# Kernel for two hybrid transformer layers on one core: seven slots instead of six in the ring of projection weights, with one piece each of q and v handled ahead

## The reference, cut to what matters

```
h = rms_norm(x, norm_g)
z = h @ w_in                         # 1024 x 3624
q, k, v, ga, qi, wi, ki, ub, gb, cv, cg, gc = split_columns(z)
q, k = partial_rope(rms_norm(q)), partial_rope(rms_norm(k))
uc = cv * sigmoid(cg)
att  = attention over the top 132 keys (64 for samples), chosen by
       sum_h wi * relu(qi . ki)       # 8 index heads of 32
pool = windowed means of ub, minus ub, times pool_w
conv = silu(layer_norm(31-tap depthwise conv(uc)))
x = x + concat(att * silu(ga), pool * silu(gb), conv * silu(gc)) @ w_out
```

## Time and profile before

| | us |
|---|---|
| median of 3 runs | 876.19 (873.66 to 878.19) |
| the profiled execution | 876.71 |
| its span, first to last instruction | 875.4 |
| TensorE busy (share of the span) | 805.3 (92%) |
| VectorE busy | 609.3 (70%) |
| ScalarE busy | 328.0 (37%) |
| POOL busy | 333.1 (38%) |

### The profile page before, as it was taken

One profiled execution on the slowest core, in us unless ns is written; L12 is line 12 of the kernel. 1 busy time (PEld: TensorE's weight loads), 2 busy tenths in 40 slices (PEclk: granted clock), 3 DMA queues, 4 the chain that ended last, 5 costly groups with the idle time before them and its releaser, 6 DMA issues. The chain is left out here.

```text
span 875.4 us, 13288 instructions
## 1 busy us (share of the span) xinstructions
PE 805.3 (92%) x4620; PEld 637.6 (73%) x4620; DVE 609.3 (70%) x1432; ACT 328.0 (37%) x830; POOL 333.1 (38%) x317
## 2 busy tenths in 40 slices
PE   5898989999889899999998899899998889999998
PEld 4894635568767777789998655455877777678998
DVE  3546997999998974433444879989999898531122
ACT  3735335336653331223132444343484524122102
POOL 0033886934744700110110568886274373000000
PEclk9999989999889998999999999999999899799999
DMA  4533040314143633012134304002414154400212
GB/s 166 154 99 100 16 121 13 84 42 124 49 113 94 203 124 123 1 44 81 61 101 113 100 4 121 24 21 83 144 52 106 53 163 143 144 1 23 71 54 98
DMA packets 57283, 75.09 MB, mean 86 GB/s; under 512 B 13233, under 2 KB 32889, under 8 KB 57185
## 3 DMA queue, kind: packets, MB, share of 16 engines
q1 hardware_dynamic: 57106, 74.17, 27.7%
q10 hardware_dynamic: 111, 0.08, 0.0%
HBM read 67.26 MB, written 7.61 MB: 86 GB/s over the span
## 5 line engine op out<-in xcount | busy, mean ns | idle before, releaser
L1164 PE MATMUL R<-x_hi,W_r 128*128 128x268 f32 x448 | 141.1, 315 | 27.2 <-DVE yT L1668 7.9
L1148 PE MATMUL R<-W_r,x_hi 128*128 128x512 f32 (+3 forms) x320 | 127.8, 399 | 12.2 <-DVE W_r L1474 12.2
L1177 PE MATMUL R<-yT,W 128*128 128x268 f32 (+2 forms) x768 | 135.0, 335 | 2.4 <-DVE yT L1474 2.4
L1166 PE MATMUL R<-x_hi,W_r 128*128 128x268 f32 x448 | 136.0, 304 | 0.0
L1165 PE MATMUL R<-x_lo,W_r 128*128 128x268 f32 x448 | 135.7, 303 | 0.0
L1177 PEld LDWEIGHTS R<-yT,W 128*128 128x128 f32 x768 | 114.8, 201 | 16.0 <-DVE yT L1474 2.6
L1149 PE MATMUL R<-W_r,x_hi 128*128 128x512 f32 (+3 forms) x320 | 120.7, 377 | 0.0
L1164 PEld LDWEIGHTS R<-x_hi,W_r 128*128 128x128 f32 x448 | 92.2, 206 | 38.9 <-DVE yT L1668 11.9
L1150 PE MATMUL R<-W_r,x_lo 128*128 128x512 f32 (+3 forms) x320 | 120.3, 376 | 0.0
L1474 DVE SCALAR_TENSOR_TENSOR cc<-uext,params,cc 128x528 f32<-128x528 f32 x120 | 110.4, 965 | 0.0
L764 POOL TENSOR_TENSOR W_r<-W,W_r 128x1024 fp32r<-128x1024 f32 x28 | 66.4, 2380 | 88.8 <-ACT W_r L882 88.6
(11 more groups left out here) (232 smaller groups left out, 1408.5 us busy)
## 6 DMA issues: line engine op xcount, KB each, us to landing
W<-in_w_in SPq DMA_DIRECT2D x52, 512.0 KB, 4.2
KV<-in_cache_k SPq DMA_DIRECT2D x32, 256.0 KB, 2.8
W<-in_w_out SPq DMA_DIRECT2D x8, 1024.0 KB, 7.4
KV<-in_cache_v SPq DMA_DIRECT2D x32, 256.0 KB, 2.8
ubx<-qkv_rows SPq DMA_DIRECT2D x16, 256.0 KB, 3.7
zi<-z_rows SPq DMA_DIRECT2D x16, 196.0 KB, 3.6
W<-in_w_in SPq DMA_DIRECT2D x8, 296.0 KB, 3.4
out_new_k_prompt<-kz SPq DMA_DIRECT2D x8, 256.0 KB, 2.0
```

Source lines behind the costliest of these rows:

```text
L1148: pe.matmul(out, x_hi[:, kc, rows], hi, start=(kc == 0), stop=False)
L1164: pe.matmul(out, hi[:, cols], x_hi[:, kc, toks], start=(kc == 0), stop=False)
L1166: m = pe.matmul(out, lo[:, cols], x_hi[:, kc, toks], start=False, stop=(kc == KC - 1))
L1177: m = pe.matmul(R[:, k, 0:hi - lo], W[:, slot(x), kc % 4, 128 * (u[1] % 4):128 * (u[1] % 4) + 128], yT[:, kc, lo:hi], start=(kc == 0), sto ...
```

## The change

The ring has seven slots instead of six. The load of piece m then waits for piece m - 7, so each batch that SP issues holds the pieces one further on. On ScalarE, high(14) moves from behind k's tile 4 to behind tile 2, and high(18) from behind q's tile 4 to behind tile 3. On VectorE, rest(14) moves from behind the k loop to behind tile 3 of it, and rest(18) likewise in the q loop. `w_out` lies in slots 3 to 6, so the waits in front of layer 1's first loads name other pieces, and the wait in front of pieces 0 and 1 names ga1, the last user of slots 0 and 1, instead of gc.

```diff
@@ -64,7 +64,7 @@
 
 LOADS = [(g, q) for g in range(len(GROUPS)) for q in range(SLOTS_OF[g])] + [(len(GROUPS) + g, q) for g in range(2) for q in range(2)]
 LOAD_OF = {x: m for m, x in enumerate(LOADS)}
-W_SLOTS = 6
+W_SLOTS = 7
 
 
 def slot(m):
@@ -605,10 +605,10 @@
 
             def w_first():
 
-                for m in range(AHEAD, 6):
-                    if l and m < 4:
+                for m in range(AHEAD, W_SLOTS):
+                    if l and AHEAD < m < 5:
                         sp.wait_ge(*unit_s.at(NUM["out", 3, 2] + 1 - len(UNITS)))
-                    elif l:
+                    elif l and m >= 5:
                         sp.wait_ge(*unit_s.at(0))
                     w_load(m)
 
@@ -632,8 +632,8 @@
                 pw_s.did(sp.dma_start(pwb[lo:lo + 64, g // 2, lo:lo + 64], dr(l, "pool_w")[:, g].rearrange("a i o -> (a i) o")))
             if l:
                 w_first()
-            w_load(6)
             w_load(7)
+            w_load(8)
             for n in range(N_SAMPLE * N_PAGES):
                 kic_s.did(sp.dma_start(kic[:, n // N_PAGES, n % N_PAGES, :],
                                        a["cache_kidx"][l:l + 1, bass.ds(pages[n], 1)].rearrange("a b p d -> (a b p) d")))
@@ -641,7 +641,7 @@
                 sp.wait_ge(*spv_s.at(0))
             for n in range(4):
                 kv_load(n)
-            for m in range(8, 14):
+            for m in range(9, 15):
                 w_load(m)
             for i in range(NT):
 
@@ -661,13 +661,13 @@
 
             for i in range(2):
                 k_store(i)
-            for m in range(14, 18):
+            for m in range(15, 19):
                 w_load(m)
             for i in range(2, NT):
                 k_store(i)
             sp.wait_ge(*kz_s.at(NT + 1))
             row_q.did(sp.dma_start(qkv_dram[0], kz[0:8, NT % 3, :]))
-            for m in range(18, 22):
+            for m in range(19, 23):
                 w_load(m)
 
             def v_store(i):
@@ -682,10 +682,9 @@
 
             for i in range(4):
                 v_store(i)
-            for m in range(22, 26):
+            for m in range(23, 27):
                 w_load(m)
             v_store(4)
-            w_load(26)
             w_load(27)
 
             sp.wait_ge(*nst_k.at(4))
@@ -731,7 +730,7 @@
                 w_load(m)
 
             if l + 1 < DEPTH:
-                wait_unit(sp, LAST_UNIT[G["gc"]])
+                wait_unit(sp, LAST_UNIT[G["ga1"]])
                 for m in range(AHEAD):
                     next_w.did(sp.dma_start(w_raw(m), w_source(l + 1, m)))
             for n in range(16, 32):
@@ -981,8 +980,9 @@
                 if i == 0:
                     high(12)
                     high(13)
+                if i == 2:
+                    high(14)
                 if i == 4:
-                    high(14)
                     high(15)
                 if i >= 2:
                     kq_keep(i - 2)
@@ -994,8 +994,9 @@
                 if i == 1:
                     high(16)
                     high(17)
+                if i == 3:
+                    high(18)
                 if i == 4:
-                    high(18)
                     high(19)
                 kq_keep(3 + i)
             for i in range(NT):
@@ -1616,7 +1617,8 @@
                         tap(j)
                         j += 1
                 kq_sum(i)
-            rest(14)
+                if i == 3:
+                    rest(14)
             rest(15)
             for i in range(NT):
                 for x in range(IX_Q):
@@ -1626,9 +1628,10 @@
                         tap(j)
                         j += 1
                 kq_sum(NT + i)
+                if i == 3:
+                    rest(18)
                 if i < 4:
                     topk_round((1, 2))
-            rest(18)
             rest(19)
             topk_round((1, 2))
             assert j == CONV_W and p == len(PIECES) and acc_s.n == ACC_END
```

## The result

The changed kernel took 885.22 us (median of 15 runs, 877.58 to 895.43) beside 878.19 us for the kernel before on the same chip (15 runs, 870.39 to 886.87): ratio 1.0077, 95% interval 1.0043 to 1.0111, 0.8% slower. The profiled execution took 885.22 us, its span 883.9 us; the mean granted clock is 0.926, before it was 0.945. The ratios of this document leave out runs more than 1.5% above the fastest of their kernel. Since the time of a run follows its granted clock, means over all runs stand beside them where it matters.

The account below looks back on a forecast made before the run. TensorE sets the time on average, but VectorE's backlog causes the 12.2 us of split waits. Gains of 2.8 + 1.8 + 2 x 0.3 = 5.2 us from 876.71 give 871.5, said as 871.0; range 866.0 to 876.4.

Parts of the forecast that it names:

- The wait at q 0: Unit q 0: the 4.07 us stall before chunk 4 becomes 2.8 us before chunk 6; lead 2.8 us, layer 1 1.8.
- waits for relu: Sign of being wrong: TensorE waiting for ScalarE's relu in the q units.
- The rival by which the wait goes altogether: Splits at q 0 and v: both waits and the half speed go, capped by VectorE's idle time, 864.9 us; chance 0.09.
- idle time that VectorE was to give up: Sign of being right, layer 0, k to q: VectorE's 5.6 us idle between 134.9 and 153 falls by 2 to 4.
- A slow stretch like the present one would take 1.3 of them: Layer 1's q 0: half speed takes 1.3 of the 2.5 us lead, giving the low end 1.2 us.
- as long as now: Layer 0's q 0: half speed lasting until about 134.9 as before leaves a lead of 1.8 us, the low end.
- q to v: Unit v 0: the 1.47 us stall moves to chunk 6; net gain 0.3 us a layer, range 0 to 0.5.
- what is queued behind (stores of k and v, the cache pages) moves by nothing: SP's load queue: later loads stand one place earlier in their batch, but stores and cache pages behind them do not move.
- cost and gain are 0: Seventh slot: the loads ended none of TensorE's listed waits, so loading pieces earlier gains and costs 0.
- The contention that I had bounded: Moved rest passes on VectorE beside POOL's work: no extra taken, upper end 0.8 us a layer.
- A lead won before 153 therefore passes through: After layer 0's k to q stage: a lead that TensorE and VectorE both have lasts, limited by VectorE's idle time.
- The third rival: Half speed follows v 0's longer stall, 2.7 us a layer; layer 1's q 0 loses 0.8; 880.0 us, chance 0.08.

Follow-up runs that it names:

- e2: The changed kernel with POOL's page products held back until VectorE's five diagonal passes are done (the hold); 883.07 us, ratio 1.0040 to the kernel before.
- e8: Ring of seven slots with no split moved, POOL's page products held until VectorE's five diagonals are done; 881.50 us, ratio 1.0047 to the kernel before.
- e7: The whole change, but TensorE waits in front of chunk 4 of q 0 for the splits of pieces 14 and 15 both; 886.42 us, ratio 1.0125.

## Why the prediction was wrong

The forecast was 871.0 us, 866.0 to 876.4, with 0.08 for slower. It took 885.2.

- **The wait at q 0: right.** Pass 15 ends when it did, the wait is 2.62 us (2.8 forecast) in front of chunk 6 in both layers, and the waits for the split went to 7.9 us in 4 (9 to 10 in 4). Of the 4.3 us saved there, 1.0 came back as waits for relu, two of them new, in the q units, where the prediction had named them as a sign of being wrong. The rival by which the wait goes altogether is out. Of the 2 to 4 us of idle time that VectorE was to give up between 134.9 and 153, 0.8 went (5.58 to 4.74), as TensorE had little lead left there to ask for it.
- **The clock behind it: the step that failed first.** "A slow stretch like the present one would take 1.3 of them" was the lower bound for layer 1, and half speed "as long as now" the lower bound for layer 0. The bound was no bound. Layer 1 had 13.7 us of half speed instead of 3.4, and instead of a lead of 1.8 us a loss of 3.3; layer 0's lead of 2.6 us at 131.46 had shrunk to 0.5 by the time full speed was back. I took the length of the slow stretch as a thing that follows the length of the stall, 4.07 us bringing more than 2.8. The runs show stalls of 2.6 us with up to 17.1 us of half speed, stalls of 4.1 us with 3.4, and the offset between stall's end and the clock's fall as what goes with it.
- **q to v: right, somewhat small.** One wait of 1.32 us where 1.5 to 2 was said, full speed, a lead of 0.9 in each layer instead of 0.3.
- **"what is queued behind (stores of k and v, the cache pages) moves by nothing", "cost and gain are 0": wrong.** I checked the batches of loads behind which stores stand, and not the load of piece 29 in front of the sample rows, whose wait the ring also eases. The gain of 4 us for POOL was the cost: its products met VectorE's diagonals, 3.06 us more of VectorE's time there, then 13.7 us of half speed instead of 6.8. What that costs the whole kernel stays open, as the hold gave nothing in e2 and e8. The contention that I had bounded (0.8 us a layer, for the moved passes) did not come; the passes took 1.41 us a pair at 116.09. I looked for it at the moved instructions only.
- **The price of half speed elsewhere: not in the sum at all.** 3.2 us of the profiled loss lie in layer 1's output stage, more than 100 us behind the last moved split and the meeting. The ring also lets layer 1's four loads of `w_out` go out within 2.3 us from 730.41, where they took 23.4 us from 724.09; but TensorE has no wait over 0.2 us between 800 and 861, so these loads are not the loss. "A lead won before 153 therefore passes through" assumed that the stages behind take the same time from wherever they begin. They don't: their clock depends on it.
- **The third rival** (the clock turns it slower, 880.0) had the right cause and sign, mostly at the wrong place: v 0 never left full speed. Its term for layer 1's q 0, 0.8 us lost, pointed the right way; 3.3 were lost. I gave it 0.08 because the matmuls behind the stalls of v were at full speed, which was true and said nothing about q 0.

Shown: the extra half speed, its four places, what it costs (0.37 us for each us), that the meeting goes with the longer stretch behind it, that a tap without any moved split does the same at q 0. The rule of the offset is read out of 38 layers and was not predicted by an experiment that held (theory D, its first form, fell). Open: what makes the output stage fall into its series, and so why the ring alone, which has the meeting too, comes out fastest. Its work is only 1.2 us shorter by the table; the other 3 us are clock. None of the four output stages in its two profiles has the series (one has two of its four stretches), and no run here sets that at will.

## What to carry to other kernels

Price a change that shifts TensorE's waits with two numbers, the work it removes and the half-speed time of the whole span, and compare versions by many runs with their granted clock; a few us of work less can be buried under 20 us more at 1.2 GHz in stages that were not touched. When a resource grows, follow each wait that it eases, also those of later loads, to what stands behind it in the queue, and ask what that will now run beside. Here the version to keep is the ring of seven without the moved splits (medians 873.7 and 874.8 us in two sets of runs, mean 4.2 us below the kernel before), or the change with one tap moved and POOL held (mean 874.9).

## What was not expected of the hardware

TensorE ran at half speed through 12 us of matmuls with hardly a gap (552.39 to 566.04), and in 3.4 us stretches that came again with every item of an output stage without a wait. The Trainium skill, "TensorE: Matmul & The Clock Gate", section "What's actually happening", says that the chip judges activity on a raster that runs free of the kernel; the two bunches of runs of e7, 7 us apart, fit it but don't show it. Its section "HAM oscillation — how this bites in real kernels" ties the loss to long idle gaps; here stalls of 2.6 us and stretches with none had it.
